# Two-block model on one core: where the decay chain and two gates of the recurrence stand in four instruction streams

## The reference, cut to what matters

```python
p = (u @ w_in)                       # 256 x 3344, split into pool, HGRN, RWKV and GLA parts
# HGRN: gated linear attention, then a gate
y_hgrn = rms_norm(o_h, hgrn_norm) * sigmoid(hg)
# RWKV: the decay and the rate of a recurrence over tokens
w_log = -softplus(-(rwkv_w0 + tanh(xw) @ rwkv_w2)) - 0.5
decay = exp(-exp(w_log))
a     = sigmoid(rwkv_a0 + xa @ rwkv_a2)
g_r   = sigmoid(xg) @ rwkv_g2
S_t = S_{t-1} diag(w_t) - (S_{t-1} kk_t)(kk_t * a_t)^T + v_t k_t^T ;  o_t = S_t r_t
# GLA: gated linear attention with normalised heads, then another gate
y_gla = o_g * gla_norm * silu(gg)
y = concatenate([y_pool, y_hgrn, y_rwkv, y_gla]) @ w_out
```

## Time and profile before

| | |
|---|---|
| median of three executions | 1637.36 us (1635.53 to 1638.42) |
| profiled execution | 1635.96 us, of which the span takes 1634.2 us |
| TensorE busy | 1573.5 us (96%) |
| VectorE busy | 1204.2 us (74%) |
| ScalarE busy | 864.9 us (53%) |
| GpSimd busy | 116.5 us (7%) |
| chain that ended last | PE 80%, DVE 10%, ACT 5%, issue 3%, DMA 1% |
| mean granted TensorE clock | 0.989 of full |

### The profile page before, as it was taken

One profiled execution on the slowest core, in us unless ns is written; L12 is line 12 of the kernel. 1 busy time (PEld: TensorE's weight loads), 2 busy tenths in 40 slices (PEclk: granted clock), 3 DMA queues, 4 the chain that ended last, 5 costly groups with the idle time before them and its releaser, 6 DMA issues.

```text
span 1634.2 us, 24767 instructions
## 1 busy us (share of the span) xinstructions
PE 1573.5 (96%) x10292; PEld 1357.7 (83%) x10292; DVE 1204.2 (74%) x1428; ACT 864.9 (53%) x1009; POOL 116.5 (7%) x138
## 2 busy tenths in 40 slices
PE   7999999989999999998999999999999999999998
PEld 7999989877999989956999986578877878878776
DVE  6767769755777776455777763659889988988996
ACT  5343456443443344345433342557777677777775
POOL 0100012210000000061000001700000000000000
PEclk9999999989999999999999999999999999999999
DMA  8877634212687764504777750039898988988983
GB/s 344 296 272 271 242 111 148 72 72 80 262 322 297 280 241 155 181 1 171 298 259 277 272 194 0 1 104 366 341 349 315 379 318 315 373 328 312 370 329 138
DMA packets 51922, 386.32 MB, mean 236 GB/s; under 512 B 5888, under 2 KB 6224, under 8 KB 7904
## 3 DMA queue, kind: packets, MB, share of 16 engines
q1 hardware_dynamic: 50400, 376.16, 61.9%
q0 software_dynamic: 1408, 8.54, 1.4%
HBM read 383.63 MB, written 1.05 MB: 235 GB/s over the span
## 4 chain that ended last, share of the span: by engine, by line
PE 80%; DVE 10%; ACT 5%; issue 3%; DMA 1%; POOL 0%; DVEq 0%; ACTq 0%; SPq 0%
PE bank L302 22%; PE bank L304 21%; PE bank L303 21%; PE bank L1289 4%; DVE sb_wlo L2295 2%; PE bank L1864 2%; ACT sb_whi L2289 2%; PE bank L1823 1%; DVE sb_wlo L269 1%; PE bank L1854 1%; DMA sb_ada_raw<-in_ada 1%; PE bank L699 1%; PE bank L2024 1%; ACT sb_whi L265 1%; PE bank L1984 1%
## 5 line engine op out<-in xcount | busy, mean ns | idle before, releaser
L269 DVE TENSOR_TENSOR sb_wlo<-sb_raw,sb_whi 128x2048 fp32r<-128x2048 f32 x137 | 313.8, 2292 | 169.7 <-ACT sb_whi L265 169.4
L302 PE MATMUL bank<-sb_xhi,sb_whi 128*128 128x256 f32 x1344 | 382.1, 284 | 4.9 <-DVE sb_xlo L585 2.8
L303 PE MATMUL bank<-sb_xlo,sb_whi 128*128 128x256 f32 x1344 | 380.3, 283 | 0.0
L304 PE MATMUL bank<-sb_xhi,sb_wlo 128*128 128x256 f32 x1344 | 380.3, 283 | 0.0
L265 ACT ACTIVATE sb_whi<-sb_raw 128x2048 fp32r<-128x2048 f32 x137 | 261.4, 1908 | 175.7 <-PE bank L304 172.1
L302 PEld LDWEIGHTS bank<-sb_xhi,sb_whi 128*128 128x128 f32 x1344 | 257.8, 192 | 9.2 <-issue 5.3
L303 PEld LDWEIGHTS bank<-sb_xlo,sb_whi 128*128 128x128 f32 x1344 | 257.8, 192 | 1.1
L304 PEld LDWEIGHTS bank<-sb_xhi,sb_wlo 128*128 128x128 f32 x1344 | 257.8, 192 | 0.0
L2295 DVE TENSOR_TENSOR sb_wlo<-sb_raw,sb_whi 128x2048 fp32r<-128x2048 f32 x84 | 191.4, 2286 | 14.6 <-ACT sb_whi L2289 13.4
L302 PE MATMUL bank<-sb_whi,sb_slots_hi 128*128 128x512 f32 x448 | 180.8, 404 | 0.0
L304 PE MATMUL bank<-sb_whi,sb_slots_lo 128*128 128x512 f32 x448 | 176.2, 393 | 0.0
(11 more groups left out here) (462 smaller groups left out, 2488.5 us busy)
## 6 DMA issues: line engine op xcount, KB each, us to landing
sb_raw<-in_ffn SPq DMA_DIRECT2D x98, 1024.0 KB, 4.9
sb_raw<-in_moe SPq DMA_DIRECT2D x86, 1024.0 KB, 5.6
sb_ada_raw<-in_ada SPq DMA_DIRECT2D x32, 1536.0 KB, 6.3
sb_cst<-in_moe SPq DMA_DIRECT2D x28, 1024.0 KB, 5.6
sb_xn<-in_moe SPq DMA_DIRECT2D x27, 1024.0 KB, 6.3
sb_ada_raw<-in_moe SPq DMA_DIRECT2D x27, 1024.0 KB, 5.8
sb_raw<-in_w_in SPq DMA_DIRECT2D x13, 1024.0 KB, 4.8
sb_raw<-in_na_qk SPq DMA_DIRECT2D x8, 1024.0 KB, 5.4
```

The lines of the kernel that those rows point to most:

```text
L269: e.tensor_tensor(wlo[s][:, :], raw[s][:, :], whi[s][:, :], ALU.subtract).then_inc(s_lo[s], 1)
L302: e.matmul(dst, wh, xh, start=first, stop=False, skip_group_check=skip)
L303: e.matmul(dst, wh, xl, start=False, stop=False, skip_group_check=skip)
L304: return e.matmul(dst, wl, xh, start=False, stop=last, skip_group_check=skip)
```

## The change

1. `rwkv()` no longer waits for the second to last chunk's result (`held[4]`) but for an earlier one (`held[8]`). Its square root, tanh and sigmoid move up one step of `between`.
2. The four `lora` matmuls write banks 2 and 3, which the GLA attention has left, in place of banks 4 + slot, and come a step later than the tanh; they now wait for the sigmoid of `xg` too. The sigmoids of their results follow in the same step, and the decay chain on DVE in the next.
3. The sigmoid of `hg` (128x512) and the gate of GLA move into `others()`, ahead of the copy `rwkv_g`. The gate is no longer a Silu but a second sigmoid, written to `hi_`, and a product on POOL.
4. The copy of `kc` waits for that product.

```diff
-            while 4 not in held:
+            while 8 not in held:
                 yield
             lo_in, xg = rw[:, 6, :], rw[:, 7, :]
             lent["roots"] = AC(heads[:, 0, :], bank[3][:, 0:NB * MH], ACT.Sqrt, m_sum)
             m4 = AC(lo_in[0:64, :], lo_in[0:64, :], ACT.Tanh, held[8])
             lent["xg"] = AC(xg, xg, ACT.Sigmoid, held[8])
-            (s_w, _, _), (s_a, _, _) = env["split_ahead"]
-            b_w, b_a = bank[4 + s_w], bank[4 + s_a]
-            lent["banks"] = b_w, b_a, bank[4 + 3 - s_w - s_a]
-            pe.wait(held[12], held[4], *w_lora)
+            yield
+            b_w, b_a = bank[2], bank[3]
+            pe.wait(*w_lora)
             for i in range(GT):
-                m6 = MM(b_w[:, i * T:(i + 1) * T], lora[:, 0, i * P:(i + 1) * P], lo_in, True, True, m4)
+                m6 = MM(b_w[:, i * T:(i + 1) * T], lora[:, 0, i * P:(i + 1) * P], lo_in, True, True, m4, lent["xg"])
...
-            own["gate_ready"] = AC(hg, hg, ACT.Sigmoid, held[4])
             lent["decays"], lent["rates"] = m6, m7
             yield
...
-        for z in (streams[0], streams[0], streams[1], streams[0]):
+        for z in streams * 4:
             next(z, None)
+        (s_w, _, _), (s_a, _, _) = env["split_ahead"]
+        lent["banks"] = bank[4 + s_w], bank[4 + s_a], bank[4 + 3 - s_w - s_a]
+        pe.wait(held[12], held[4])
...
+                own["gate_ready"] = AC(hg, hg, ACT.Sigmoid, held[4])
+                m = AC(hi_, gg, ACT.Sigmoid, held[12])
+                lent["gate_ready"] = TT(pool, gg, gg, hi_, ALU.mult, m)
+                m_table = AC(heads[:, 1, 0:1], env["epss"][:, 0:1], ACT.Sqrt)
                 m = AC(g[:, :, :], b_o[:, :].rearrange("p (k t) -> p k t", k=2), ACT.Copy, m8)
...
-                lent["gate_ready"] = AC(gg, gg, ACT.Silu, held[12])
-                m_table = AC(heads[:, 1, 0:1], env["epss"][:, 0:1], ACT.Sqrt)
                 yield
...
-                outs["kc"] = m = AC(kct, blocks(b_o[:, :]), ACT.Copy, m)
+                outs["kc"] = m = AC(kct, blocks(b_o[:, :]), ACT.Copy, m, lent["gate_ready"])
```

## The result

The changed kernel takes 1643.92 us (median of seven executions, 1642.10 to 1644.67), the kernel before, beside it, 1637.73 us (seven, 1635.53 to 1641.51). The ratio is 1.0032, 95% interval 1.0022 to 1.0042: slower by more than the 0.2% that counts as no change. The two medians alone differ by 6.19 us, which would be 1.0038; by the ratio it is 5.2 us. The profiled execution took 1644.67 us.

The account below looks back on a forecast made before the run. TensorE, busy 96% of the 1634.2 us span, was taken as the bound, so only its waits and half clock count. Terms 4.7 - 3.0 = +1.7 on the 1637.36 median gave 1639.1 us, counted as no change; range 1635.6 to 1643.5.

Parts of the forecast that it names:

- ScalarE's queue: ScalarE from the exponential at 312.75: sigmoid of xg ends at 318.3, whi0 runs to 323.4, last exponential ends at 325.8.
- TensorE's `lora` matmuls: Low-rank matmuls behind the last chunk: start at 318.35, 3.2 us earlier, after a 0.9 us wait, at full clock.
- The first term: Decay branch up to the product with tok: +4.7 us, the chain waiting in DVE's queue for whi0 and the last exponential.
- The second term: Gates ahead of rwkv_g: the 1.49 us wait before the ada_raw matmuls and half clock behind it go, -3.0 us.
- the term's other 1.47: Matmuls behind the ada_raw wait: 3.42 us at half level become 1.95 at full level, saving 1.47 us.
- A: Rival after 343 us: DVE's queue ends last, so early gates give nothing; +4.7 us, 1642.1 us, chance 0.16.
- B: Rival: clock returns later after longer idle, slowing 5.72 us of matmuls from 337.53; +4.7, 1642.1 us, chance 0.12.
- C: Rival: kinder clock, half level ends before the product with tok and is missed at 384-388; -2.4, 1635.0 us, chance 0.11.
- D: Rival on ScalarE: each table switch costs another 1.4 us beyond its load; +4.4, 1641.8 us, chance 0.02.
- My bound on the first term, 6.3: Upper bound for the decay branch's delay, 6.3 us, if the lora matmuls still run at half clock.
- the lower one, 4.2: Lower bound for the decay branch's delay, 4.2 us, if the product into ex0 runs without POOL beside it.

Follow-up runs that it names:

- pool_late: Changed kernel with GpSimd's two copies of the unit blocks also waiting for the end of the decay chain; 1640.79 us, ratio 1.0016 to the kernel before.
- before_again: The kernel before, unchanged, run and profiled again for the spread; 1638.97 us, ratio 1.0001.
- after_again: The changed kernel, unchanged, run and profiled again; 1644.64 us, ratio 1.0027 to the kernel before.
- chain_only: Changed kernel with the gates put back, leaving the moved tanh, lora matmuls and decay chain; 1643.32 us, ratio 1.0025 to the kernel before.
- gates_only: Kernel before with only the gates' two sigmoids, product and table load moved ahead of rwkv_g; 1639.06 us, ratio 0.9998.
- gates_again: Repeat of the kernel before with only the gates' part moved ahead of rwkv_g; 1637.97 us, ratio 0.9992.
- root_again: Kernel before with the gates moved and the square root behind the sigmoids of the rates, a repeat; 1634.69 us, ratio 0.9959.
- root_only: Kernel before with one edit, the square root moved behind the sigmoids of the rates, gates unmoved; 1635.55 us, ratio 0.9959.

## Why the prediction was wrong in the time, and right in the order

**ScalarE's queue: right.** Three tables and functions were to end 5.55 us behind the exponential and ended 5.58 behind it (320.95 less 315.37). `whi0` was forecast at 8.75 and came at 8.61, the end of the last exponential at 13.05 and came at 12.94.

**TensorE's `lora` matmuls: right.** Expected at +5.6, at full clock, with a wait of 0.9; measured +5.72, 1.00 granted and 1.96 us for all eight, 0.94.

**The first term: the mechanism right, the size too small.** Forecast +4.7; `tok` moved from 15.83 to 21.74, +5.91. Up to the start of the decay chain I was 0.64 us too late: 13.95 forecast, 13.31 measured (328.68 less 315.37), because the product into `ex0` took 0.42 and not 0.94: it now starts 0.05 us ahead of GpSimd's product `qd`, where it had started 1.33 behind it. The failed step is the chain's 3.11 us, which I carried over unchanged: it took 4.88, so +1.77. The scale went from 0.43 to 0.95 and the two running sums from 1.27 to 2.53; of these the first took 1.95, beside the copies, and the second, behind them, 0.66. GpSimd's product `qd` and its two copies stand one behind the other in a queue of their own, and `qd` waits for the last exponential; the prediction followed what is pushed back on ScalarE, VectorE and TensorE, and not on GpSimd. Before, the copies ran at 320.82 and 321.37, beside VectorE's picks, which they don't slow. pool_late shows 1.24 us of it by itself: without the copies beside the chain `tok` stands at 20.50, which is where the prediction's sum had put it (333.25 less 312.75). Against before_again, where it stands at 15.22, the move of `tok` is 6.5 us and not 5.9: the `lora` matmuls at half level had cost the first trace 0.6.

The Trainium skill, "SBUF — State Buffer", in its practical consequences, says that a VectorE instruction with two SBUF inputs contends with a GpSimd instruction that reads SBUF, and that tensor_scalar can too. I had weighed that rule for the new GpSimd product and the product into `ex0`, and not for the chain. The trace agrees with it for the running sums (two SBUF inputs, 2.53 in place of 1.27) and for the scale.

**The second term: right in the stretch, hardly in the time.** Forecast −2.96; between the bonus matmuls and the transposes 6.04 us (345.03 to 351.07) became 2.98 (353.56 to 356.54), −3.06. Nothing else in the stretch lost it again: its length is +2.87, and 5.91 − 3.06 is 2.85. But the time of the kernel rose by 5.2 us (0.0032 of 1637.73), and by 4.4 in after_again. The first term alone, chain_only, costs 4.1 us in time (2.0 to 6.1 by its interval), which holds the 4.7 of the forecast and the 5.9 of the trace. So the sum failed a second time, at the step that takes every microsecond gained in this stretch as one of the time.

Four pairs of kernels on one chip differ by the gates alone: gates_only and gates_again against before, after_again against chain_only, root_again against root_only. Their stretches are 3.0, 3.3, 4.4 and 2.0 us shorter. By the means of all their executions, the spans differ by −0.3, −1.3, +0.9 and −0.1 us, together −0.4 with a 95% interval of about −1.2 to +0.5. That excludes the gains of the stretches.

The record has the mean granted clock of each of these executions, and with it the missing part can be placed roughly. The product of span and clock counts each microsecond at half level as half (an estimate: idle time at half level counts so too, and the clock is recorded to three digits). It is lower by 1.2, 1.3, 1.4 and 2.1 us in the four pairs, together 1.5 (0.8 to 2.2). The rest of the span, what the half level adds, is +0.8, −0.1, +2.3 and +2.0. So by this estimate something of the size of the wait of 1.49 us is gained in each pair. What stands for the half level behind it (the term's other 1.47) is not: the half level costs as much as before, or more, at other places.

That piece at half level was not the wait's doing alone either. Behind the same wait of 1.49 us the 32 matmuls take 1.93 us in the trace of before, 1.68 in before_again and 1.63 in chain_only, but 1.15, the full level, in root_only, where bonus matmuls and transposes are 4.53 us apart and not 6.04. In the same way the prediction ascribed the half level of `lora` to their wait of 2.96 us, and before_again and gates_again have that wait and the full level behind it. That −3.06 came so near to −2.96 is partly luck, then. The nine traces with the gates moved all have the 32 matmuls at full level, but what that gains depends on the trace beside them: −2.80 from before_again to after_again, −1.56 from root_only to root_again.

**What is open.** Why the cost of the half level does not shrink with the wait, and where it goes. In the profiled pair the span is 8.7 us longer, and it splits into 2.62 before the stretch, 2.87 in it and about 3.2 behind it. The parts outside have the same instructions, but their clock falls in other places. One window of the kernel before, and the same of the kernel after, whose work stands 1.15 us later there (the granted clock is the figure before the last two):

```profile
239.00:245.00 6.00, 5.44 (x52) 5.35 (x53) 5.97 (x9) 4.67 (x6) 2.05 (x1) 1.00 0.20 44
```

```profile
239.00:245.00 6.00, 4.29 (x30) 4.10 (x31) 5.93 (x9) 4.68 (x6) 2.05 (x1) 0.72 0.06 11
```

Such pieces come and go between traces of one kernel, and what is left of the span outside the stretch differs by 3.9 and 3.6 us between the repeats. No run moves such a piece on purpose, so no cause is shown.

**The rivals.** A said that the second term fails because VectorE ends last; its time, 1642.1 (B's is the same), is the nearest to what was measured, but its mechanism did not occur: the wait is gone and VectorE's, 0.48, is as before. B, the clock back later: from `tok` to the bonus matmuls it is 16.45 us in both traces (328.58 to 345.03, 337.11 to 353.56), and the half level ends some 5.5 us behind the start of `tok` in both. C: the idle time did not spare the clock, and the time shows no gain. D, a price of the switch beyond its load: again 4.93 us for three loads and functions.

**The range.** The median, 1643.92, lies 0.4 us above its upper end; the ratio applied to the 1637.36 of the forecast gives 1642.6, inside it. The change counted as none in the forecast, at +1.7 us, and was slower by 5.2. The upper end took rival A and B singly at +4.7 us; with a first term of 5.9 and no second the time would be 1643.3, near the measured one. My bound on the first term, 6.3, held it, but stood for another case, the `lora` matmuls at half clock; the lower one, 4.2, had the product into `ex0` without POOL beside it, which is what came; POOL's copies I had at nothing.

## What to carry to other kernels

When a step is moved up in a queue, follow what is pushed back on every engine, the small helpers too: an operation that was harmless beside one kind of VectorE work can double another. Look at which ScalarE functions share a table before moving anything: taking the square root out from between exp and tanh removed a load without moving the chain, and that one line gained 0.41%, where the whole change lost 0.32%. And a gain of 3 us read in one trace of a program whose clock moves by as much from run to run is a gain only once it stands in the times.

## What the runs showed of the hardware that I had not expected

- Two TENSOR_TENSOR_SCAN of 128x256 with two SBUF inputs take 1.27 us; with GpSimd's copies from SBUF beside the first of them they take 2.53, that one 1.95 and the next 0.66. The first is recorded as starting 0.22 us ahead of the first copy, and was held all the same. A TENSOR_SCALAR of 128x512 goes from 0.43 to 0.95 beside GpSimd's product `qd`. COPY_PREDICATED from PSUM keeps its 1.32 beside the same copies.
- A GpSimd product of 128x512 beside VectorE work that reads a bank takes 1.27 us, where I had reckoned 1.5. The product into `ex0` took 0.42 us when it started 0.05 ahead of GpSimd's `qd` and 0.94 when it started 1.33 behind it, and `qd` then 0.96 and 1.99.
- TensorE keeps the level of 2.4 GHz over an idle 0.94 us and loses it in one of 10.88 us; the mean over 324 to 335 is 0.74. Between these, one and the same idle time is followed by either level: 2.96 us ahead of `lora` by half in before and by full in before_again, 1.49 us ahead of the `ada_raw` matmuls by half in before and by full in root_only. The length of an idle time alone does not tell the level behind it.
